# First output projection moved from a phase of its own into the steps of forgetting attention and time mixing

## What is computed

```python
    ya = spatial_gating(a_u, a_v, sgu_norm_g, sgu_w, sgu_b)
    ...
    yb = forgetting_attention(b_q, b_k, b_v, b_f + fox_f_b, fox_q_g, fox_k_g)
    ...
    yc = mlstm(c_qk, c_v, c_i + mlstm_i_b, c_f + mlstm_f_b, c_o, mlstm_conv_w, mlstm_conv_b, mlstm_out_g)
    ...
    yd = rwkv7_time_mix(d_r, d_wlo, d_k, d_v, d_alo, rwkv_w0, rwkv_w2, rwkv_a0, rwkv_a2,
                        rwkv_k_k, rwkv_k_a, rwkv_r_k, rwkv_ln_g)
    ...
    ym = memory_attention(m_q, rms_norm(mem, mem_norm_g), mem_w_kv, mem_q_g, mem_k_g)
    branches = [(ya, a_z), (yb, b_z), (yc, c_z), (yd, d_z), (ym, m_z)]
    mixed = jnp.concatenate([y.astype(x.dtype) * jax.nn.silu(z) for y, z in branches], axis=-1)
    return x + mixed @ w_out
```

## Time and profile before

| | us |
|---|---|
| time, median of 3 runs | 5201.58 (5184.79 to 5215.15) |
| span of the profiled execution | 5189.6 |
| first phases, to the preparing steps | 0 to 1209 |
| preparing steps | 1209 to 1349 |
| steps k = 0 and 1 | 1349 to 1461.3 |
| steps k = 2 to 15 | 1461.3 to 2471 |
| steps k = 16 and 17, to the last operation | 2471 to 2488.3 |
| `project_out`, to the first operation behind it | 2488.3 to 2744.6 |
| `second_projection` and the second layer | 2744.6 to 5189.6 |

### The profile page before, as it was taken

One profiled execution on the slowest core, in us unless ns is written; L12 is line 12 of the kernel. 1 busy time (PEld: TensorE's weight loads), 2 busy tenths in 40 slices (PEclk: granted clock), 3 DMA queues, 4 the chain that ended last, 5 costly groups with the idle time before them and its releaser, 6 DMA issues. The chain is left out here.

```text
span 5189.6 us, 65192 instructions
## 1 busy us (share of the span) xinstructions
PE 4361.9 (84%) x23554; PEld 3247.0 (63%) x23554; DVE 2639.9 (51%) x5371; ACT 1922.0 (37%) x3900; POOL 711.8 (14%) x745
## 2 busy tenths in 40 slices
PE   7997999984688888888898999977787878787679
PEld 6885777774566555656787888853344444454467
DVE  3113444445555544444212111138889888888545
ACT  3112323324323333333101101023667776777621
POOL 3102111100000000000000000003222333344400
PEclk9998999985567777778899999976677788778789
DMA  5327666664000000000423212120000000101033
GB/s 184 119 106 239 210 221 204 215 206 139 28 24 24 24 24 24 13 24 3 154 109 115 82 65 81 55 73 17 19 28 29 19 19 19 37 19 35 31 126 118
DMA packets 203393, 425.84 MB, mean 82 GB/s; under 512 B 37224, under 2 KB 67596, under 8 KB 202908
## 3 DMA queue, kind: packets, MB, share of 16 engines
q1 hardware_dynamic: 203072, 421.67, 23.7%
HBM read 299.93 MB, written 121.65 MB: 81 GB/s over the span
## 5 line engine op out<-in xcount | busy, mean ns | idle before, releaser
L3185 POOL TENSOR_TENSOR ds_E<-ds_bT 128x256 f32<-128x256 f32 x112 | 72.8, 650 | 2797.5 <-ACT ds_bT L3154 2620.6
L2718 PE MATMUL ds_big<-ds_ikT,ds_iqT 64*128 64x512 f32 (+3 forms) x608 | 382.0, 759 | 75.4 <-ACT ds_iqT L2695 54.6
L301 PE MATMUL g_acc<-g_ws_hi,g_hT_hi 128*128 128x512 f32 (+1 forms) x1024 | 386.5, 377 | 0.0
L303 PE MATMUL g_acc<-g_ws_hi,g_hT_lo 128*128 128x512 f32 (+1 forms) x1024 | 384.9, 376 | 0.0
L302 PE MATMUL g_acc<-g_ws_lo,g_hT_hi 128*128 128x512 f32 (+1 forms) x1024 | 384.9, 376 | 0.0
L529 PE MATMUL mm_big<-mm_gw_hi,mm_ghT_hi 128*128 128x512 f32 (+1 forms) x768 | 321.4, 418 | 31.0 <-PEq L134 31.0
L2774 DVE TENSOR_SCALAR_CACHE_REDUCE ds_seen<-ds_eq,ds_num 128x2048 uint16<-128x2048 uint16 (+13 forms) x224 | 331.3, 1479 | 26.4 <-issue 4.4
L531 PE MATMUL mm_big<-mm_gw_hi,mm_ghT_lo 128*128 128x512 f32 (+1 forms) x768 | 302.7, 394 | 0.0
L530 PE MATMUL mm_big<-mm_gw_lo,mm_ghT_hi 128*128 128x512 f32 (+1 forms) x768 | 302.0, 393 | 0.0
L2814 ACT ACTIVATE ds_signs<-ds_lo,ds_at 128x2048 bf16<-128x2048 uint16 (+13 forms) x224 | 291.3, 1301 | 1.5
L328 DVE COPY g_stage<-g_acc 128x512 f32<-128x512 f32 (+1 forms) x64 | 41.5, 649 | 459.2 <-PE g_acc L303 459.2
(11 more groups left out here) (519 smaller groups left out, 10155.1 us busy)
## 6 DMA issues: line engine op xcount, KB each, us to landing
mm_ghT_hi<-turned SPq DMA_DIRECT2D x96, 512.0 KB, 3.8
mm_ghT_lo<-turned SPq DMA_DIRECT2D x96, 512.0 KB, 5.5
proj<-g_stage SPq DMA_DIRECT2D x112, 256.0 KB, 2.0
proj<-mm_gstage SPq DMA_DIRECT2D x80, 256.0 KB, 5.0
mm_x<-proj SPq DMA_DIRECT2D x64, 256.0 KB, 3.8
second_raw<-in_w_in SPq DMA_DIRECT2D x56, 256.0 KB, 4.2
proj<-fp_stage SPq DMA_DIRECT2D x48, 256.0 KB, 2.0
mm_graw<-in_w_in SPq DMA_DIRECT2D x40, 256.0 KB, 6.4
```

The source lines that it names most:

```text
L301: pe.matmul(sums, hT.hi[:, k, tile], wt.hi[:, k, 0:width], start=(k == 0), stop=False)
L303: mm = pe.matmul(sums, hT.lo[:, k, tile], wt.hi[:, k, 0:width], start=False, stop=(k == KD - 1))
L2718: pe.matmul(big[:, n % 2, 0:wd], iqT[o, h // 2], b.ikT[o, x:x + wd], start=True, stop=True)\
```

## The change

`project_out` is no longer called for the first layer. In its place:

- Steps 0 and 1 (`out_split`) load five blocks of `w_out` each, split them on ACT (high) and POOL (low), and store both halves in a DRAM array `halves`.
- Steps 2 to 17 (`out_product` of tile k - 2) load the tile's part of `mixed` (the time mixing's own part is taken from its SBUF tile), turn it in three groups (4, 4 and 2 transposes, each through ACT and DVE before the next, since all use bank 4), and do the same 60 matmuls, in two passes of 30 over 512 output columns. The split weights come back from `halves` in 40 pieces of 256 KB through a ring of 7 slots. The sum is added to `x` by DVE in two halves and stored in the next step.
- To free bank 4, `rwkv_back` uses one bank, with its state as two 128 x 128 blocks. To free SBUF, the queries go to DRAM in the preparing steps (`queries`) and return tile by tile; half of the keys lie in `raw`; `pv` has one buffer and its load waits for `shifted`. Step 16 issues the load of `raw` for the next phase.

Cut to its core (the places where the like is done again are left out):

```diff
-def fox_rwkv_and_gating(nc, c, w, proj, mixed):
+def fox_rwkv_and_gating(nc, c, w, proj, mixed, q_d, split_d, x_out, raw):
...
-        qT = B.sb("qT", [A, HEADS, SEQ])
-        kT = B.sb("kT", [A, HEADS, SEQ])
+        kT = [raw[0:A].rearrange("p k n -> p (k n)").rearrange("p (h t) -> p h t", h=2), B.sb("kT", [A, 2, SEQ])]
         v = B.sb("v", [P, TILES, GW])
...
+        ob = out_buffers(B, big, rb, w, mixed, split_d, x_out)
...
+            if k < 2:
+                names += OUT_SPLIT_SIGNALS
+            else:
+                names += OUT_SIGNALS
+            if k == TILES:
+                names += "raw_in "
...
+                if k < 2:
+                    branches.append(out_split(ob, s, k))
+                else:
+                    branches.append(out_product(c, ob, s, k - 2))
...
+                    if k == TILES:
+                        for j in range(KD):
+                            sp.dma_start(raw[:, j], w['w_in_2'][j * P:(j + 1) * P, 0:512]).then_inc(s.raw_in, 16)
...
+OUT_K = MIX1 // P
+OUT_SLOTS = 7
+OUT_GROUPS = [(0, 4), (4, 4), (8, 2)]
+OUT_ROWS = [0, 1, 2, 3, 4, 5, 8, 9, 6, 7]
+OUT_SPLIT_SIGNALS = "os_in0 os_in1 os_hi os_lo os_out0 os_out1 "
+OUT_SIGNALS = "om_in ox_in ox_stored ox_last o_turned o_hi o_lo o_used o_added " + "".join(
+    f"ow_in{n} " for n in range(OUT_SLOTS))
+def out_buffers(B, big, rb, w, mixed, split_d, x_out):
+    b = Named()
+    b.bank, b.rb, b.mixed, b.split_d, b.x_old, b.x_out, b.w_out = big[:, 4], rb, mixed, split_d, w['x'], x_out, w['w_out']
+    b.mS = Split(B, "mS", [P, OUT_K, P])
+    b.m = B.sb("om", [P, 4 * GW])
+    b.x = B.sb("ox", [P, D_MODEL])
+    b.wr = B.sb("ow", [P, OUT_SLOTS, 512], F32R)
+    return b
...
+def out_split(b, s, k):
+    rows = range(k * OUT_K // 2, (k + 1) * OUT_K // 2)
+    raw = (b.x[:].rearrange("p (n c) -> p n c", n=2), b.m[:].rearrange("p (n c) -> p n c", n=2))
+    hi = (b.wr[:, 0:2], b.wr[:, 2:4])
+    lo = (b.wr[:, 4:6], b.mS.lo[:, 0:8].rearrange("p (n k) c -> p n (k c)", n=2))
+    arrived, out = (s.os_in0, s.os_in1), (s.os_out0, s.os_out1)
+    at = lambda j: 0.02 + 0.18 * j
+    def sync(sp):
+        for j, r in enumerate(rows):
+            yield at(j)
+            if j >= 2:
+                sp.wait_ge(s.os_lo, j - 1)
+            sp.dma_start(raw[j % 2], b.w_out[r * P:(r + 1) * P, :].rearrange("p (n c) -> p n c", n=2))\
+              .then_inc(arrived[j % 2], 16)
+            if j:
+                yield at(j) + 0.01
+                keep(sp, j - 1)
+        yield 0.96
+        keep(sp, len(rows) - 1)
+        yield 1.0
+        for a in range(2):
+            sp.wait_ge(out[a], 32 * len(rows[a::2]))
+    def keep(sp, j):
+        sp.wait_ge(s.os_lo, j + 1)
+        for a, half in enumerate((hi, lo)):
+            sp.dma_start(b.split_d[rows[j], a].rearrange("p (n c) -> p n c", n=2), half[j % 2].bitcast(F32))\
+              .then_inc(out[j % 2], 16)
+    def scalar(act):
+        for j in range(len(rows)):
+            yield at(j) + 0.06
+            act.wait_ge(arrived[j % 2], 16 * (j // 2 + 1))
+            if j >= 2:
+                act.wait_ge(out[j % 2], 32 * (j // 2))
+            act.activation(hi[j % 2], raw[j % 2], ACT.Copy).then_inc(s.os_hi, 1)
+    def gpsimd(pool):
+        for j in range(len(rows)):
+            yield at(j) + 0.08
+            pool.wait_ge(s.os_hi, j + 1)
+            pool.tensor_tensor(lo[j % 2], raw[j % 2], hi[j % 2].bitcast(F32), ALU.subtract).then_inc(s.os_lo, 1)
+    return {"sync": sync, "scalar": scalar, "gpsimd": gpsimd}
...
+def out_product(c, b, s, t):
+    tok = slice(t * P, (t + 1) * P)
+    mS, m, x, wr, bank = b.mS, b.m, b.x, b.wr, b.bank
+    own = b.rb.y[:, t % 2].rearrange("p h d -> p (h d)")
+    arrived = [(s.ow_in0, s.ow_in1, s.ow_in2, s.ow_in3, s.ow_in4, s.ow_in5, s.ow_in6)[n] for n in range(OUT_SLOTS)]
+    slices = [(n, j, a) for n in range(2) for j in range(OUT_K) for a in range(2)]
+    halves = x[:].rearrange("p (n c) -> p n c", n=2)
+    at_turn = lambda g: 0.07 + 0.045 * g
+    at = lambda n, j: 0.22 + 0.39 * n + 0.34 * j / OUT_K
+    cols = lambda n: slice(n * 512, (n + 1) * 512)
+    def sync(sp):
+        yield 0.0
+        sp.dma_start(m[:, 0:3 * GW], b.mixed[tok, 0:3 * GW]).then_inc(s.om_in, 16)
+        sp.dma_start(m[:, 3 * GW:4 * GW], b.mixed[tok, 4 * GW:5 * GW]).then_inc(s.om_in, 16)
+        if t:
+            sp.dma_start(b.x_out[(t - 1) * P:t * P, :], x[:]).then_inc(s.ox_stored, 16)
+        for q in range(OUT_SLOTS):
+            weights(sp, q)
+        yield 0.1
+        if t:
+            sp.wait_ge(s.ox_stored, 16)
+        sp.dma_start(x[:], b.x_old[tok, :]).then_inc(s.ox_in, 16)
+        for q in range(OUT_SLOTS, len(slices)):
+            n, j, a = slices[q - OUT_SLOTS]
+            yield at(n, j + 0.5 * a + 0.5)
+            sp.wait_ge(s.o_used, q - OUT_SLOTS + 1)
+            weights(sp, q)
+        if t == TILES - 1:
+            yield 1.1
+            sp.wait_ge(s.o_added, 2)
+            sp.dma_start(b.x_out[tok, :], x[:]).then_inc(s.ox_last, 16)
+            sp.wait_ge(s.ox_last, 16)
+    def weights(sp, q):
+        n, j, a = slices[q]
+        sp.dma_start(wr[:, q % OUT_SLOTS].bitcast(F32), b.split_d[OUT_ROWS[j], a, :, cols(n)])\
+          .then_inc(arrived[q % OUT_SLOTS], 16)
+    def tensor(pe):
+        for g, (j0, n) in enumerate(OUT_GROUPS):
+            yield at_turn(g)
+            if g == 0:
+                pe.wait_ge(s.om_in, 32)
+            else:
+                pe.wait_ge(s.o_lo, g)
+            for j in range(n):
+                src = m[:, (j0 + j) * P:(j0 + j + 1) * P] if j0 < 8 else own[:, j * P:(j + 1) * P]
+                p = pe.transpose(bank[:, j * P:(j + 1) * P], src, c.ident)
+            p.then_inc(s.o_turned, 1)
+        for n in range(2):
+            for j in range(OUT_K):
+                q = (n * OUT_K + j) * 2
+                yield at(n, j)
+                if j == 0 and n == 0:
+                    pe.wait_ge(s.o_lo, len(OUT_GROUPS))
+                elif j == 0:
+                    pe.wait_ge(s.o_added, 1)
+                pe.wait_ge(arrived[q % OUT_SLOTS], 16 * (q // OUT_SLOTS + 1))
+                whi, wlo = wr[:, q % OUT_SLOTS], wr[:, (q + 1) % OUT_SLOTS]
+                pe.matmul(bank, mS.hi[:, j], whi, start=(j == 0), stop=False)
+                pe.matmul(bank, mS.lo[:, j], whi, start=False, stop=False).then_inc(s.o_used, 1)
+                pe.wait_ge(arrived[(q + 1) % OUT_SLOTS], 16 * ((q + 1) // OUT_SLOTS + 1))
+                pe.matmul(bank, mS.hi[:, j], wlo, start=False, stop=(j == OUT_K - 1)).then_inc(s.o_used, 1)
+    def scalar(act):
+        for g, (j0, n) in enumerate(OUT_GROUPS):
+            yield at_turn(g) + 0.012
+            act.wait_ge(s.o_turned, g + 1)
+            act.activation(mS.hi[:, j0:j0 + n], bank[:, 0:n * P].rearrange("p (k t) -> p k t", t=P), ACT.Copy)\
+               .then_inc(s.o_hi, 1)
+    def vector(dve):
+        for g, (j0, n) in enumerate(OUT_GROUPS):
+            yield at_turn(g) + 0.022
+            dve.wait_ge(s.o_hi, g + 1)
+            dve.tensor_tensor(mS.lo[:, j0:j0 + n], bank[:, 0:n * P].rearrange("p (k t) -> p k t", t=P),
+                              mS.hi[:, j0:j0 + n].bitcast(F32), ALU.subtract).then_inc(s.o_lo, 1)
+        for n in range(2):
+            yield at(n, OUT_K) + 0.01
+            dve.wait_ge(s.o_used, 2 * OUT_K * (n + 1))
+            if n == 0:
+                dve.wait_ge(s.ox_in, 16)
+            dve.tensor_tensor(halves[:, n], halves[:, n], bank, ALU.add).then_inc(s.o_added, 1)
+    return {"sync": sync, "tensor": tensor, "scalar": scalar, "vector": vector}
...
+            sp.dma_start(b.q[:, (k + 1) % 2], b.q_d[k + 1]).then_inc(s.z_ahead, 16)
             yield 0.9
-            sp.wait_ge(s.z_ahead, 16)
...
-                    pe.matmul(big[:, n, 0:wd], b.qT[:, h, k * P:(k + 1) * P], b.kT[:, h, x:x + wd], start=True,
+                    pe.matmul(big[:, n, 0:wd], b.q[:, k % 2, h], b.kT[h // 2][:, h % 2, x:x + wd], start=True,
...
+    def sync(sp):
+        for u in range(U):
+            yield at(u) + 0.15
+            sp.wait_ge(s.q_kept, u + 1)
+            sp.dma_start(b.q_d[i * U + u], qs[:, u]).then_inc(s.q_out, 16)
+        yield 1.0
+        sp.wait_ge(s.q_out, 16 * U)
...
-            dve.tensor_copy(kT[:, :, (i * U + u) * P:(i * U + u + 1) * P], tp[0:A, 1]).then_inc(s.k_kept, 1)
+            for j in range(2):
+                d = dve.tensor_copy(kT[j][:, :, (i * U + u) * P:(i * U + u + 1) * P], tp[0:A, 1, 2 * j:2 * j + 2])
+            d.then_inc(s.k_kept, 1)
...
-    b.pv = B.sb("pv", [P, 2, D_W])
+    b.pv = B.sb("pv", [P, D_W])
...
-def rwkv_loads(b, sp, arrived, proj, i):
+def rwkv_loads(b, sp, arrived, proj, i, free=None):
     sp.dma_start(b.x[:, i % 3], proj[i * P + PAD:(i + 1) * P + PAD, D_0:D_0 + D_W]).then_inc(arrived, 16)
-    sp.dma_start(b.pv[:, i % 2], proj[i * P + PAD - 1:(i + 1) * P + PAD - 1, D_0:D_0 + D_W]).then_inc(arrived, 16)
+    if free is not None:
+        sp.wait_ge(free, 1)
...
```

(24 more changed lines are left out.)

70 lines of the change are left out of this document (42 added, 28 removed).

## The result

The changed kernel takes 5115.2 us (median of 4 runs, 5112.1 to 5116.6) against 5204.6 (median of 4, 5184.8 to 5215.2) for the kernel before, run beside it: a ratio of 0.9845, 95% interval 0.9826 to 0.9863. That is 89 us less, where the forecast was 30 (5172 against 5201.6). The profiled execution has a span of 5112.9 us, 77 less than before, and a mean clock of 0.845.

| stage | before, us | forecast, us | after, us | after less forecast |
|---|---|---|---|---|
| first phases | 1209.0 | 1209.0 | 1212.4 | +3.5 |
| preparing steps | 140.1 | 146.1 | 154.4 | +8.2 |
| steps 0 and 1 | 112.3 | 122.3 | 114.0 | -8.3 |
| steps 2 to 15 | 1009.7 | 1141.3 | 1099.5 | -41.8 |
| step 16 | 17.3 | 50 | 53.4 | +3.4 |

The account below looks back on a forecast made before the run. PE was taken as the bound, at a slow clock in steps 2 to 15. Removing 256.3 us and adding 78.7, 131.6, 10 and 6 gave -30.0 on a 5189.6 span, plus 12 to the median: 5172 us, range 5095 to 5265.

Parts of the forecast that it names:

- `rwkv_back` has fewer and wider matmuls, 0.5 less: Steps 2 to 15: fewer and wider matmuls in `rwkv_back` save 0.5 us a step.
- 60 matmuls: Steps 2 to 15: a tile's 512-column matmuls cost 13.6 us at full clock plus 2.4 for early slow ones, 16.0 a step.
- transposes on PE: Head of steps 2 to 15: 10 transposes at half clock, 2.6 us a step.
- old work faster: Steps 2 to 15: about 12 of 39 us at half clock turn to full clock, 4.5 us a step won.
- idle time (filled, head, slices): Steps 2 to 15, per step: 6 us of PE's waits filled, 1.3 added by ACT and DVE at the head, 0.5 by late slices.
- the splitting: Steps 0 and 1: ACT copies of the high halves in the chain of `rwkv_front` cost 10 us in all (4 to 16).
- rounded 6: Preparing steps: halved copies into `kT` cost 2.4 us and the last queries' store 3, rounded 6 (1 to 10).
- The 300 GB/s: Steps 16 and 17: the assumed rate of the uncovered weight stream, giving 50 and 46 us.
- Slices late: Steps 2 to 15: waits for a late weight slice cost 0.5 us a step.
- clock as now (0.73): Rival for steps 2 to 15: clock does not rise, 18.1 us a step, time 5293; chance 0.22 with little better included.
- stream as the bound: Rival: weight pieces bring only 170 GB/s, steps 2 to 7 and the last two lengthen, 5270 us; chance 0.08 with its waits.
- The rival of a full clock from the first trio on: Rival for steps 2 to 15: full clock from the first product matmuls, 4.0 us a step, time 5096; chance 0.2.

Follow-up runs that it names:

- the kernel of one bank: Kernel before the change with only `rwkv_back` put into one bank, its state as two 128 x 128 blocks: 5151.3 us, ratio 0.9919.
- 512 columns in a row: Changed kernel with only 7 weight slices loaded and each half tile's 30 matmuls in one row: 5190.6 us, ratio 0.9994 to the kernel before.
- 64 columns in the waits: Changed kernel with each product matmul cut from 512 to 64 columns, places and loads kept: 5168.9 us, ratio 0.9955 to the kernel before.
- The repaired order: Changed kernel with the gating's store ahead of the last queries' store in the preparing steps: 5102.2 us, ratio 0.9827 to the kernel before.

## Why the prediction was right and wrong

The direction held, and so did the mechanism in the main: the product went into waits of PE, and the time at half clock fell as forecast. The size did not. The forecast gain was 30 us, the measured one 89, three times as much. The time lay in the wide range (5095 to 5265), but under the 5130 to 5215 to which the forecast gave its 0.5, and 57 us under the forecast. Of these 57, 47 are the sum of the last column of the table, and 10 are the distance from span to median: I added 12 as before, and it was 2.

**The step that failed** is the term "`rwkv_back` has fewer and wider matmuls, 0.5 less", a size put in without a row. With that edit alone the steps lost 2.1 us each, 30 us in the 14 where the term gave 7, and 5 more in steps 0 and 1, for which the sum had no such term. That is 28 of the 47 us by which the span fell short of the forecast. Of the 77 us that the span lost in all, 35 go with an edit made only to free a bank (41 of 89 by the medians of whole runs). The products of `rwkv_back` were in the trace of before and could have been priced from it. Of the other 19 us, 12 lie behind the change and have no known cause, and the rest is the balance of the terms below.

**Steps 2 to 15, per step**, forecast and measured, with the kernel of one bank as the base of the product's terms (before one bank took its 2.1):

| term | forecast | measured |
|---|---|---|
| 60 matmuls | 16.0 | 18.9 |
| transposes on PE | 2.6 | 2.5 |
| old work faster | -4.5 | -7.9 |
| idle time (filled, head, slices) | -4.2 | -4.9 |
| `rwkv_back` | -0.5 | -2.1 |
| sum | 9.4 | 6.4 |

The measured terms are: 264.6 and 34.4 us by start to next start; PE's busy time less these, against the 822.2 of one bank; idle time from the windows; 979.8 against 1009.7. Matmuls and old work are to be read together, 11.0 against 11.5: at the border of a long and a short matmul the time falls to the one or the other by the way of counting. In that pair the sum was good to 0.5 us. Whether its two parts missed by 3 us each and cancelled, or only the counting differs, no run here separates. The half clock came out as forecast (27 us a step), but 4 of the 12 us came with one bank and 8 with the product; by the factor of 1.65 these 8 are 3.2 us, not 4.5. The reason given there, wide products, was half of it: 512 columns in a row left 33 us, 64 columns in the waits 47.

**Steps 0 and 1**: the splitting cost 6.3 us over the kernel with one bank (107.7), where 10 were forecast; the 4.6 that one bank gives there left 1.7.

**The preparing steps**: "rounded 6" was 14. The argument saw one landing, at the last step, and half-width copies. It went through the new stores but not through SP's queue behind them: each of the four steps with queries ended with two landings in a row. The repaired order took 10 to 12 us off.

**Steps 16 and 17**: 50 and 46 against 53.4 and 46.6. The 300 GB/s were 271. The missed part is `raw` ahead of `mixed` on SP, 8.2 us of PE standing, which is hidden in part since bytes are the bound.

**Slices late**: 0.5 a step was 0. **The rivals**: clock as now (0.73) is excluded, stream as the bound too. The rival of a full clock from the first trio on gave 5096 and was nearer than the forecast in time, but not in mechanism: it had 4.0 us a step from 20 us at half clock; these were 27, and with the 0.5 that it too had for `rwkv_back` the steps would have come to 8.0 and not 6.4. Of the signs listed, the trios at 0.23 us a matmul in the levels failed: they took 0.36, 0.23 and 0.29 on average at full clock.

**The rest of the kernel** took 12.4 us less, with no edit in it. The three profiled kernels that have the projection in a phase of its own took 2442 to 2448 us there, the eleven with the product in the steps 2431 to 2440. The granted clock goes with it: 0.833 to 0.835 in the three, 0.839 to 0.848 in the eleven. The same 500 us of work in the second layer, before and after:

```profile
4000.00:4500.00 500.00, 403.23 (x1681) 240.30 (x1682) 434.82 (x843) 363.43 (x699) 163.57 (x187) 0.80 0.07 24
3936.00:4436.00 500.00, 394.54 (x1718) 238.27 (x1717) 439.38 (x854) 366.19 (x711) 166.99 (x189) 0.83 0.07 23
```

From 0.835 to 0.844 the half clock falls by 42 us in this stage, an estimate of 16 us by the factor of 1.65, enough for the 12. Why the clock there should differ with the place of an earlier phase stays open.

## What to carry to other kernels

Price every edit that a change needs as carefully as the change itself: one that only freed a bank shortened every step by 2 us here. When work is put into waits, give PE wide matmuls there, a few at each wait. Here narrow ones filled the time at a lower clock than none (0.71 against 0.75), and the same wide ones in a row left the waits open and the half clock near that of none (33 and 35 us a step). After adding a store with a wait, read the in-order queue behind it to the step's end, and where a stage is bound by weights, let two tiles share them.

## What the runs showed of the hardware

- Taking work out made the kernel slower: with 64 of 512 columns the steps lasted 1123 us, with 512 1099, with 256 1049. Granted clock 0.71, 0.83, 0.80; without these matmuls 980 us at 0.75.
- The first of three 512-column matmuls between short ones took 0.36 us on average to the next start at full clock (0.34 in the median), the second 0.23, the last 0.29 (0.32 in the median), where each takes 0.226 in a row.
- A stream of 256 KB blocks that raised the DMA rate from 63 to 174 GB/s beside PE at 92% busy changed the length of these 14 steps by nothing that can be seen (1100.8 without it, 1099.5 us with it). In the last steps, which such blocks bind, all DMAs together moved 271 to 274 GB/s.
